# A hand-ordered expert loop: down weights converted later, gate of the next expert ahead of the small down product

## The reference

```python
def expert_block(args):
    xblk, e = args
    hdn = jax.nn.silu(xblk @ w_gate[e]) * (xblk @ w_up[e])
    return hdn @ w_down[e]
```

## Time and profile before

| | before |
|---|---|
| median of 3 executions | 1103.8 us (1103.5 to 1105.72) |
| the profiled execution | 1105.72 us, span 1104.0 us |
| mean granted TensorE clock | 0.972 |
| PE busy | 1040.3 us, 94% of the span |
| VectorE, ScalarE, GpSimd busy | 572.6, 450.0, 170.6 us |
| data moved | 288.28 MB, mean 261 GB/s |

### The profile page before, as it was taken

How to read it: one execution, slowest core, us unless ns; L and a number is a source line. 1 busy time by engine, 2 the same in 40 slices (tenths; PEclk the granted TensorE clock), 3 DMA queues, 4 the chain that set the end, 5 groups by cost and what they waited for, 6 DMA issues and landing times.

```text
span 1104.0 us, 14465 instructions
## 1 busy us (share of the span) xinstructions
PE 1040.3 (94%) x5009; PEld 748.8 (68%) x5009; DVE 572.6 (52%) x1021; ACT 450.0 (41%) x593; POOL 170.6 (15%) x201
## 2 busy tenths in 40 slices
PE   8999999999999999988799999999999998999985
PEld 7778899788888787877466555665465654656652
DVE  4320422144557787777464663445544545545568
ACT  5312221224335410045345564454544545545644
POOL 3000111000000000012114221142123231323100
PEclk9999999999999999998989999999999998999998
DMA  8612314722123322157999999999999999999684
GB/s 308 229 53 101 124 44 131 239 62 77 39 73 121 114 78 77 58 194 304 344 417 420 420 414 409 408 414 388 386 412 413 377 395 364 411 420 401 254 368 185
DMA packets 71451, 288.28 MB, mean 261 GB/s; under 512 B 14319, under 2 KB 22639, under 8 KB 45796
## 3 DMA queue, kind: packets, MB, share of 16 engines
q1 hardware_dynamic: 60320, 258.34, 59.8%
q0 software_dynamic: 9920, 25.04, 6.0%
q10 hardware_dynamic: 1156, 4.20, 0.9%
HBM read 262.73 MB, written 33.82 MB: 269 GB/s over the span
## 4 chain that ended last, share of the span: by engine, by line
PE 62%; DMA 23%; DVE 6%; issue 3%; ACT 3%; DVEq 2%; SPq 0%; POOL 0%; POOLq 0%; ACTq 0%
PE bank L1829 14%; PE bank L1831 14%; PE bank L1830 14%; DMA raw_b<-l_w_down 12%; DMA raw<-l_w_gate 7%; PE bank L2233 5%; ACT whi L918 2%; PE bank L2251 2%; PE bank L2014 1%; PE bank L2016 1%; DMA yy<-expert_rows 1%; PE bank L2063 1%; PE bank L2019 1%; DMA raw_up<-l_w_up 1%; PE bank L2175 1%
## 5 line engine op out<-in xcount | busy, mean ns | idle before, releaser
L1648 DVE TENSOR_TENSOR wlo<-raw_b,whi 128x2048 fp32r<-128x2048 f32 x64 | 146.3, 2291 | 165.5 <-ACT whi L918 165.4
L1829 PE MATMUL bank<-whi,xhi 128*128 128x512 f32 x384 | 155.4, 405 | 0.9 <-ACT num L861 0.6
L1831 PE MATMUL bank<-whi,xlo 128*128 128x512 f32 x384 | 151.1, 394 | 0.0
L1830 PE MATMUL bank<-wlo,xhi 128*128 128x512 f32 x384 | 150.9, 393 | 0.0
L918 ACT ACTIVATE whi<-raw_b 128x2048 fp32r<-128x2048 f32 x64 | 122.2, 1912 | 47.3 <-DMA raw_b<-l_w_down 46.9
L2233 PE MATMUL bank<-raw_up,xT_s 128*64 128x512 f32 x240 | 120.0, 647 | 0.0
L2234 PE MATMUL bank<-raw_s,xT_s 128*64 128x512 f32 x240 | 120.0, 647 | 0.0
L1829 PE MATMUL bank<-whi,xghi 128*128 128x512 f32 x272 | 110.9, 408 | 1.0 <-DVE xglo L1661 1.0
L1831 PE MATMUL bank<-whi,xglo 128*128 128x512 f32 x272 | 106.9, 393 | 0.0
L1648 DVE TENSOR_TENSOR lo_b<-raw,whi 128x2048 fp32r<-128x2048 f32 x32 | 73.1, 2288 | 53.7 <-ACT whi L918 53.7
L1831 PEld LDWEIGHTS bank<-whi,xlo 128*128 128x128 f32 x384 | 72.8, 190 | 16.0
(11 more groups left out here) (391 smaller groups left out, 1861.0 us busy)
## 6 DMA issues: line engine op xcount, KB each, us to landing
raw<-l_w_gate SPq DMA_DIRECT2D x32, 1024.0 KB, 17.4
raw_b<-l_w_up SPq DMA_DIRECT2D x32, 1024.0 KB, 15.9
raw_b<-l_w_down SPq DMA_DIRECT2D x32, 1024.0 KB, 14.8
raw_s<-l_w_gate SPq DMA_DIRECT2D x32, 1024.0 KB, 10.0
raw_up<-l_w_up SPq DMA_DIRECT2D x32, 1024.0 KB, 18.1
raw_down<-l_w_down SPq DMA_DIRECT2D x32, 1024.0 KB, 17.9
raw<-l_w_in SPq DMA_DIRECT2D x5, 2048.0 KB, 8.7
yy<-expert_rows SPq DMA_DIRECT2D x8, 1024.0 KB, 11.6
```

What stands on the lines that cost most here:

```text
L1648: tt(lo_b[k][:, halves(p)], src[:, halves(p)], whi[k][:, halves(p)].bitcast(F32), ALU.subtract).then_inc(e_lo[k], 1)
L1829: t.matmul(out, lh, rh, start=first, stop=False)
L1830: t.matmul(out, lh, rl, start=False, stop=False)
L1831: return t.matmul(out, ll, rh, start=False, stop=last)
```

## The change

Nothing is computed differently and no instruction is added; orders change, and one wait.

- ScalarE, in a pair: silu_large and hidden_hi come before the two halves of the down weights. The second of these halves comes behind xg_hi. hidden_small and y_large(i, 0) come behind the first gate half, and the second up half comes last, behind y_small and x_small.
- VectorE, in a pair: times_up and hidden_lo come first; the first down half follows; the second comes behind xg_lo. Some routing work of pairs 1 to 4 moves with them.
- PE: gate_large(i + 1) comes before down_small(i - 1), and down_large(n, 1) waits for `y_cp` of 2n + 1 in place of 2n.
- SyncE: the next gate weights are requested before the small down weights.
- Before the first pair and after the last one the orders follow suit.

```diff
@@ SyncE, load_pair @@
+            large = expert_at(i * 2 + 1)
+            load_large(i + 1, large, 0)
             for p in range(2):
                 load_small(i - 1, small, 2, p)
-            large = expert_at(i * 2 + 1)
-            load_large(i + 1, large, 0)
             load_large(i + 1, large, 1)
@@ ScalarE @@
         def pair(i, ahead=1):
-            hi_large(i, 2, 0)
-            hi_large(i, 2, 1)
             silu_large(i)
             hidden_hi(i)
-            hi_large(i + 1, 0, 0)
+            hi_large(i, 2, 0)
             silu_small(i - 1)
             xg_hi(i + 1)
+            hi_large(i, 2, 1)
+            hi_large(i + 1, 0, 0)
+            hidden_small(i - 1)
+            y_large(i, 0)
             hi_large(i + 1, 0, 1)
-            y_large(i, 0)
-            hidden_small(i - 1)
+            y_large(i, 1)
             hi_large(i + 1, 1, 0)
-            y_large(i, 1)
-            hi_large(i + 1, 1, 1)
             y_small(i - 1)
             if ahead:
                 x_small(i)
+            hi_large(i + 1, 1, 1)
...
         last = last_pair + 1
+        silu_large(last)
         hi_large(last, 2, 0)
+        hidden_hi(last)
         hi_large(last, 2, 1)
-        silu_large(last)
-        hidden_hi(last)
@@ VectorE @@
         lo_large(0, 1, 1)
+        for p in range(2):
+            lo_large(0, 2, p)
         lo_large(1, 0, 0)
+        times_up(0)
         lo_large(1, 0, 1)
-        times_up(0)
         xg_lo(1)
         hidden_lo(0)
-        for p in range(2):
-            lo_large(0, 2, p)
...
         def pair(i):
-            lo_large(i, 2, 0)
-            lo_large(i, 2, 1)
             times_up(i)
+            hidden_lo(i)
...
-            hidden_lo(i)
-            lo_large(i + 1, 0, 0)
+            lo_large(i, 2, 0)
             times_up_small(i - 1)
             xg_lo(i + 1)
-            lo_large(i + 1, 0, 1)
+            lo_large(i, 2, 1)
+            lo_large(i + 1, 0, 0)
...
+            lo_large(i + 1, 0, 1)
...
         last = last_pair + 1
+        times_up(last)
         lo_large(last, 2, 0)
+        hidden_lo(last)
         lo_large(last, 2, 1)
-        times_up(last)
-        hidden_lo(last)
@@ PE @@
         def down_large(n, q):
             pe.wait_ge(N["g_lo"], n + 1)
-            wait(pe, N["y_cp"], n * 2)
+            wait(pe, N["y_cp"], n * 2 + q)
...
             down_large(i, 1)
-            down_small(i - 1)
             gate_large(i + 1)
             if isinstance(i, int) and i == 5:
                 list_past_128()
+            down_small(i - 1)
             if ahead:
                 rows_small(i)
             up_large(i + 1)
```

More of the change, by code:

```diff
@@ L1706, in pair @@
                     past_128_items()
-                if i == 4:
-                    past_128_slots(0)
-            hidden_lo(i)
-            lo_large(i + 1, 0, 0)
+            lo_large(i, 2, 0)
             times_up_small(i - 1)
             xg_lo(i + 1)
-            lo_large(i + 1, 0, 1)
+            lo_large(i, 2, 1)
+            lo_large(i + 1, 0, 0)
             if isinstance(i, int):
@@ L1722, in pair @@
                 if i == 4:
-                    past_128_slots(1)
+                    past_128_slots(0)
+            lo_large(i + 1, 0, 1)
+            if isinstance(i, int) and i == 4:
+                past_128_slots(1)
             lo_large(i + 1, 1, 0)
```

## The result

| | before | after |
|---|---|---|
| median | 1103.65 us (4 runs) | 1211.9 us (4 runs, 1205.01 to 1212.85) |
| ratio to before | | 1.0971, 95% interval 1.0922 to 1.102 |
| span of the profiled execution | 1104.0 us | 1211.2 us |
| mean granted TensorE clock | 0.972 | 0.943 |

The change makes the kernel 9.7% slower. The forecast was 1218 us, with a range from 1165 to 1250.

What follows compares the result with a forecast made beforehand. The prediction took PE to set the expert loop's pace, with transfers close to their limit. Start 3.5, pair 1 1.7, pairs 2 to 14 97.5 and the end 11.8 give 114.5 on 1105.7: 1220.2, stated as 1218 us median, range 1165 to 1250.

Steps and rivals of the forecast that it cites:

- Rival 1: Expert loop: three added PE waits plus half clock behind them make a pair 41.6 us; 1218 us, chance 0.50.
- The waits: In each pair PE waits 3.7 us at down_large(i, 0), 1.1 at down_large(i, 1), 2.2 in up_large(i+1).
- The clock: PE at 1.2 GHz behind waits costs 3.2 us a pair: first 1.8, second nothing, third 1.4.
- Rival 2: Expert loop: the waits come but the clock hardly drops, pairs 38.4 us; 1169 us, chance 0.20.
- Nothing absorbs them: Each wait follows PE's own instruction just ahead, so none shrinks when another grows; 7.0 us a pair.
- The transfers are no limit: In the slower pairs, 14.1 MB a pair leaves transfers below their limit, about 340 GB/s.
- Start: Ahead of pair 1: gate_large(1) 1.4 us later, down_large(0, 1) waits 0.7, clock 1.4; 3.5 us.
- Pairs 2 to 14: Main expert loop: 13 pairs go from 34.1 to 41.6 us each; 97.5 us.
- From pair 15: Pair 15 and the last expert: added waits and clock, less clock already lost there; 11.8 us.
- Rivals 3 to 6: Loop: clock stays low, 1250 us (0.15); part of waits, 1138 (0.08); faster, 1086 (0.04); no change (0.03).
- Rival 3: Expert loop: clock stays low across the second wait, 43.6 us a pair; 1250 us, chance 0.15.
- Rival 5: Expert loop: hidden_large wait goes, pairs between PE's 31.4 and the transfers' 34.0 us; 1086 us, chance 0.04.

Runs made afterwards that it cites:

- b_copy: Changed kernel with y_large(i, 0) ahead of hidden_small on ScalarE, PE's wait on y_cp kept; 1168.93 us, ratio 1.0615 to the kernel before.
- w1_only: e_all with the second down half put back behind xg_hi and xg_lo; 1148.73 us, ratio 1.0412 to the kernel before.
- d_fill_short: Changed kernel, all waits kept, with 12 and 9 small PE matmuls filling the waits for second down and up halves; 1163.9 us, ratio 1.0561.
- e_all: Changed kernel with second down half directly behind the first, y_large(i, 0) ahead of hidden_small, second up half ahead of y_small; 1100.96 us, ratio 0.9977.
- w2_only: e_all with y_large(i, 0) put back behind hidden_small; 1100.12 us, ratio 0.9983 to the kernel before.
- g_pe: Kernel before with only PE's and SyncE's new order of gate_large and down_small; 1105.58 us, ratio 1.0015.

## Why the prediction was right

The direction, the places and the size came out: 1211.9 us against 1218. Rival 1 is what happened. The waits were right one by one; of the clock only the sum was, and that in part by luck.

- **The waits.** 3.7, 1.1 and 2.2 us late were forecast; 3.7, 1.15 and 2.3 are measured. Together with 31.4 us of PE's own work they were to make 38.4 us at the full clock; with the waits filled the pairs are 38.3 us apart.
- **The clock.** Forecast 3.2 us a pair, measured 3.1. The parts were less right than the sum: 1.8 and 1.4 us were put behind the first and third wait, and a common pair loses 1.2 and 1.6; two pairs lose 2.4 more, one loses nothing behind the first. With another rhythm the same waits would have cost another sum, as b_copy and w1_only show. Rival 2 (clock hardly drops, 1169 us) is d_fill_short in effect, 1163.9 us. The Trainium skill's sentence that for modeling the ramp penalty is under 1% of a typical kernel's span (again "TensorE: Matmul & The Clock Gate", "The HAM clock gate") stands there beside the slow matmuls at the start of a kernel. Carried over to repeated waits, as the prediction did, it would have led to rival 2; here the clock is worth 48.0 us of 1211.9, 4%, and the measurement decides.
- **Nothing absorbs them.** Right in the changed kernel: no wait grew when another was removed. Put back alone into e_all, the second was absorbed (w2_only).
- **The transfers are no limit.** Right: share 0.87, and 331 GB/s in a pair where 340 were forecast.
- **SyncE's and PE's order costs nothing.** Right (g_pe).
- **The sum by its terms**, forecast against measured in the profiled runs. Start: 3.5 against 540.64 - 538.20 = 2.4. Pair 1: 1.7 against (582.84 - 540.64) - 39.9 = 2.3. Pairs 2 to 14: 97.5 against 13 x 41.45 - 443.1 = 95.8. From pair 15: 11.8 against (1170.18 - 1121.73) - 36.9 = 11.6. The terms are close, and they add up to 112.1 us, while the spans differ by 107.2.
- **What was missed** is 4.8 us behind the down work: 1104.0 - 1058.16 = 45.8 us before, 1211.2 - 1170.18 = 41.0 after. The prediction moved that end along unchanged. VectorE's timeline has the reason, first before and then after:

```profile
1058.90 1.28 DVE L1747 SCALAR_TENSOR_TENSOR hh<-yy,wts,hh 128x1024 f32<-128x1024 f32 x1 [5.05 <-DMA yy<-expert_rows]
...
1166.16 1.28 DVE L1747 SCALAR_TENSOR_TENSOR hh<-yy,wts,hh 128x1024 f32<-128x1024 f32 x1
```

This is the first step of VectorE's last stretch, which takes 45.1 us (1104.0 - 1058.90) before and 45.0 after. Before, it waited 5.05 us for expert rows to be read back and began 0.7 us behind the end of the down work. After, the rows are there in time and it begins 4.0 us ahead of that end: 4.8 us in all.
- **Rivals 3 to 6** didn't set the time. Rival 3's 43.6 us a pair came in two pairs of 13. Rival 5's bound is what e_all shows: without the added waits the early silu gives at most 0.4%, as the transfers stand in the way.

## What to carry to other kernels

An engine that works in a fixed order turns each step into a wait for all that is listed ahead of it. When a conversion is moved, look for the instruction of the other engine that now stands between it and its user, and count from there: here two conversions and a copy ended up behind work that PE itself does directly before it needs the result. When a second resource is near its limit, the price of a wait alone says little of its price among others; test it both ways, taken out of the slow kernel and put into the fast one.

## What the runs showed of the hardware

Two waits of 2.98 us in one kernel, two pairs apart, were followed by 1.2 GHz once and by 2.4 GHz the other time, and pairs of the same work took 37.4 or 41.3 us for it. In w1_only the same was 34.9 or 37.7 us. A small matmul on the identity, float32, 128 x 128, held PE for 0.22 us in a row of 20, not for the 0.14 us that I had put down; in the profile each leaves two records.
